# Dilated attention: products of identity by identity ahead of and inside its four calls

## The reference, cut to what matters

```python
ATTN_GROUPS = ((128, 1), (512, 4), (2048, 16))    # window, dilation; 8 heads of 64 in each group
def dilated_mixer(h, cos, sin, w_q, k_sh, v_sh, w_o):
    q = apply_rope_2((h @ w_q).reshape(B, S, 3, 8, 64), cos, sin)
    for g, (window, dilation) in enumerate(ATTN_GROUPS):
        o, l = dilated_window_attention(q[:, :, g], k_sh[:, :, g], v_sh[:, :, g], window, dilation)
    wts = softmax(stack(lses), axis=0)
    o = sum(wts[..., None] * stack(outs), axis=0)
    return o.reshape(B, S, O_WIDTH) @ w_o
```

## Time and profile before

| | |
|---|---|
| median of 3 runs | 3644.28 us (3637.61 to 3644.98) |
| the profiled execution | 3640.77 us |
| its span, first to last instruction | 3639.0 us |
| TensorE busy | 3385.7 us, 93% |
| VectorE busy | 1957.4 us, 54% |
| ScalarE busy | 1400.2 us, 38% |
| DMA | 107 GB/s, mean over the span |
| mean granted TensorE clock | 0.941 of 2.4 GHz |

### The profile page before, as it was taken

How to read it: one execution, slowest core, us unless ns; L and a number is a source line. 1 busy time by engine, 2 the same in 40 slices (tenths; PEclk the granted TensorE clock), 3 DMA queues, 4 the chain that set the end, 5 groups by cost and what they waited for, 6 DMA issues and landing times.

```text
span 3639.0 us, 41894 instructions
## 1 busy us (share of the span) xinstructions
PE 3385.7 (93%) x14724; PEld 2639.8 (73%) x14724; DVE 1957.4 (54%) x3052; ACT 1400.2 (38%) x2056; POOL 384.3 (11%) x233
## 2 busy tenths in 40 slices
PE   7799898997998898999997999999999989889998
PEld 5567677775676777788875788877887767668886
DVE  4753687557536876554546543456354443455353
ACT  3443567534434666322222322233223444432221
POOL 2101032322010222200010100010001000010000
PEclk9869999998598999999999999999999999899999
DMA  3101399611011998132322232324233212013232
GB/s 114 50 1 59 105 318 317 217 50 55 1 59 58 307 318 271 50 98 91 100 64 66 74 103 88 99 70 143 92 97 117 87 35 70 24 50 101 92 95 78
DMA packets 174980, 389.59 MB, mean 107 GB/s; under 512 B 11312, under 2 KB 70064, under 8 KB 174192
## 3 DMA queue, kind: packets, MB, share of 16 engines
q1 hardware_dynamic: 173424, 377.45, 32.3%
q0 software_dynamic: 1408, 10.23, 0.8%
HBM read 381.34 MB, written 6.29 MB: 107 GB/s over the span
## 4 chain that ended last, share of the span: by engine, by line
PE 71%; DVE 12%; DMA 8%; ACT 5%; DVEq 2%; issue 2%; POOL 0%; POOLq 0%; ACTq 0%; SPq 0%
PE ps L545 18%; PE ps L547 18%; PE ps L546 18%; DMA gate_up_stage<-in_w_gu 8%; PE ps L659 4%; DVE moe_lo L1809 4%; PE ps L681 3%; PE ps L665 2%; ACT moe_hi L1048 2%; PE ps L761 2%; PE ps L636 1%; PE ps L724 1%; PE ps L627 1%; ACT w_hi L1048 1%; PE ps L829 1%
## 5 line engine op out<-in xcount | busy, mean ns | idle before, releaser
L1466 DVE TENSOR_TENSOR w_lo<-w_stage,w_hi 128x1024 fp32r<-128x1024 f32 (+3 forms) x310 | 398.3, 1287 | 833.9 <-ACT w_hi L1048 832.8
L545 PE MATMUL ps<-xs_hi,w_hi 128*128 128x512 f32 (+2 forms) x1952 | 778.9, 399 | 53.2 <-DVE w_lo L1466 17.7
L1048 ACT ACTIVATE w_hi<-w_stage 128x1024 fp32r<-128x1024 f32 (+3 forms) x350 | 382.0, 1093 | 1032.3 <-PE ps L547 1020.9
L547 PE MATMUL ps<-xs_hi,w_lo 128*128 128x512 f32 (+2 forms) x1952 | 771.2, 395 | 0.0
L546 PE MATMUL ps<-xs_lo,w_hi 128*128 128x512 f32 (+2 forms) x1952 | 771.0, 395 | 0.0
L545 PEld LDWEIGHTS ps<-xs_hi,w_hi 128*128 128x128 f32 (+2 forms) x1952 | 369.1, 189 | 155.1 <-issue 39.1
L547 PEld LDWEIGHTS ps<-xs_hi,w_lo 128*128 128x128 f32 (+2 forms) x1952 | 368.8, 189 | 85.8
L546 PEld LDWEIGHTS ps<-xs_lo,w_hi 128*128 128x128 f32 (+2 forms) x1952 | 370.0, 190 | 82.9
L1809 DVE TENSOR_TENSOR moe_lo<-gate_up_stage,moe_hi 128x1024 fp32r<-128x1024 f32 x224 | 270.1, 1246 | 125.0 <-ACT moe_hi L1048 124.6
L1048 ACT ACTIVATE moe_hi<-gate_up_stage 128x1024 fp32r<-128x1024 f32 x224 | 226.6, 1053 | 147.6 <-DMA gate_up_stage<-in_w_gu 141.2
L547 PE MATMUL ps<-h_hi,w_lo 128*128 128x512 f32 x704 | 278.1, 395 | 0.0
(11 more groups left out here) (346 smaller groups left out, 5105.5 us busy)
## 6 DMA issues: line engine op xcount, KB each, us to landing
gate_up_stage<-in_w_gu SPq DMA_DIRECT2D x112, 1024.0 KB, 5.8
w_stage<-in_f_gu SPq DMA_DIRECT2D x174, 512.0 KB, 3.6
down_stage<-in_w_dn SPq DMA_DIRECT2D x112, 512.0 KB, 6.1
w_stage<-in_f_dn SPq DMA_DIRECT2D x64, 704.0 KB, 4.0
w_stage<-in_w_in SPq DMA_DIRECT2D x30, 512.0 KB, 3.6
w_stage<-in_d_qk SPq DMA_DIRECT2D x24, 512.0 KB, 3.5
w_stage<-in_w_out SPq DMA_DIRECT2D x16, 512.0 KB, 3.5
w_stage<-in_d_v SPq DMA_DIRECT2D x12, 512.0 KB, 3.6
```

Source lines behind the costliest of these rows:

```text
L545: pe.matmul(o, lh, rh, start=start, stop=False)
L547: return pe.matmul(o, ll, rh, start=False, stop=stop)
L1048: copy = lambda o, i: nc.scalar.activation(o, i, ACT.Copy)
L1466: tt(w_lo[:, s, 0:n], stage[:, s, 0:n], w_hi[:, s, 0:n].bitcast(F32), ALU.subtract).then_inc(w_split, 1)
```

## The change

`keep_clock` gets a third argument, the width w in tiles of 128 columns; its default leaves it as it was. Three calls are added in the dilated attention, all into bank 6:

- five products ahead of each call of `attend_wide`, before the wait for `heads_ready`. At e = 0 the wait for the last `act_copied` now stands ahead of them too, since bank 6 is one of those that the turned values are copied from;
- three products behind the scores of units 0 and 1;
- one product of 256 columns in each unit, ahead of the wait for `p_norm`.

```diff
-            def keep_clock(n, b=7):
+            def keep_clock(n, b=7, w=NT):
 
                 for _ in range(n):
-                    pe.matmul(ps[:, b, :], ident[:, :], ident[:, :].unsqueeze(1).to_broadcast([P, NT, P]), start=True, stop=True)
+                    pe.matmul(ps[:, b, 0:w * P], ident[:, :], ident[:, :].unsqueeze(1).to_broadcast([P, w, P]), start=True, stop=True)
...
                 for n in range(2):
                     scores(U[n], n, D_BANKS)
+                keep_clock(3, 6)
                 for n in range(N):
                     un, nb = U[n], U[n]["W"] // P
+                    keep_clock(1, 6, 2)
                     pe.wait_ge(p_norm, d0 + n + 1)
                     transposes(un, n, dprob, 6, D_RING)
...
                                 turn(2 * L + n_v + i - 1, (i - 1) % 2, P, 6 + (i - 1) % 2)
+                        if e == 0:
+                            pe.wait_ge(act_copied, L * COPIES + n_v + 6)
+                        keep_clock(5, 6)
                         pe.wait_ge(heads_ready, n_rope + 6 * e + 6)
                         pe.wait_ge(act_copied, L * COPIES + n_v + 6)
```

## The result

| | median | runs |
|---|---|---|
| before | 3640.47 us | 12 (3634.14 to 3646.03) |
| changed | 3651.06 us | 12 (3635.92 to 3659.01) |

The ratio is 1.0031, 95% interval 1.0019 to 1.0044: 11 us slower (7 to 16). The profiled execution took 3648.63 us, its span is 3646.9 us, 7.9 more than the 3639.0 of before.

A forecast was written before the change was run, and what follows sets the result against it. TensorE, busy for 93% of the span, was taken as the bound. Added products cost 24.0 us, the held clock gives back 17.2, a net loss of 6.8; one or two falls at e = 1 make +12: 3654 us (3645 to 3663).

The forecast's parts named there:

- No slack in units 1 to 5: Middle units of each call: TensorE waits for nothing, so narrow products cost 5 x 0.43 = 2.15 us per call.
- The faster rival: Units paced by VectorE and ScalarE, narrow products in slack, five at e = 0 overlapped: -11.8 us, 3629; chance 0.05.
- The five at e = 0 exposed: Ahead of the e = 0 calls, behind the last `dv` wait: 4.3 us exposed, twice, 8.6 us; the clock holds.
- The three and one: Between first scores and first transposes: 3.0 us of products where 1.65 were idle, 1.35 us exposed per call.
- What the clock can give: All four calls at full clock without added products: 35.0 us each, 140.0 against 157.2, so 17.2 us at most.
- The clock at e = 1: Heads of the e = 1 calls: one or two falls, 6.8 us low and 3.4 lost each; forecast chance 0.62.
- The rule of the Trainium skill: Rival at e = 1: the 1.4 us gap left is harmless, clock holds, +6.8 us, 3647.6; chance 0.18.

The follow-up runs named there:

- again: The changed kernel unaltered, measured once more on one chip beside the fitted kernel: median 3648.24 us, ratio to before 1.0023.
- the fitted kernel: Against the changed kernel, products only where TensorE was idle, no more than each gap holds, none in the units: ratio to before 0.9964, later 0.9952.
- both fitted forms: The fitted kernel, and the same with one narrow product added in each of units 1 to 7; the latter's ratio to before 0.9966, later 0.9975.

## Why the prediction was right

The forecast was 3654 us (3645 to 3663) and slower; 3651.06 and 1.0031 were measured.

- **No slack in units 1 to 5.** Right: 4.24 us for a unit. This step decided the sign. The faster rival hung on slack that the earlier trace rows didn't show, and the narrow products alone made the kernel slower. Their price was put at 0.43 us and is 0.48 (4.24 - 3.76): the two records take 0.54 us from start to start, and the transposes behind them run 0.06 faster. Per call 3.1 us came, as worked out of it.
- **The five at e = 0 exposed.** Right, 4.49 us for 4.3. That the clock holds there was right in the first call and wrong in the third, where it was low from the first of the five on and they took 6.15 us. Over the profiles with these five and the three behind (changed, again, without narrow products) that is one fall in six.
- **The three and one.** Transposes 5.92 us behind the scores for 6.05: the scores of two units take 2.80 us, not 3.05. A call at the full clock is 38.96 us for 38.8.
- **What the clock can give.** 35.0 us per call was worked out for a call with no added product at the full clock; the fitted kernel has 35.00 to 35.17. This term carries the reading that all four could gain 17 us and that the products cost more than that.
- **The clock at e = 1.** One fall in the first profile, one in the second, 6.8 us low and 3.3 us lost each, for 6.8 and 3.4. With the clock held throughout the sum would be 2 x (4.49 + 38.96) + 2 x 38.97 = 164.8, +7.6 for the forecast +6.8; two falls (3.3 at e = 1, 1.7 in the five) make it 12.6, for +12.
- **One reading too high.** The prediction says that a third of each call or more is spent at 1.2 GHz. In the first call it is 10.2 of 38.4 us, a little over a quarter; no term of the sum used this.
- **The rule of the Trainium skill** ("TensorE: Matmul & The Clock Gate", section "Why this matters for your kernels", that long idle gaps bring a mid-kernel fall) would have the clock held with 1.50 us of gap left. The trace disagrees: it fell there in six of eight e = 1 calls with the five and the three (changed twice, without the narrow ones, without the five at e = 0), and in the run with 64 rows behind a gap of 1.48 us. By these rows a gap of 1.5 us can be enough.
- **By luck:** that the sum of the clock's part came out so close, 12.6 for 12. The forecast put one or two falls at e = 1 and none at e = 0. The profile has one at e = 1 and one in the five at e = 0, together 5.0 us, where one or two of the expected kind were priced at 3.4 or 6.8. The second profile, with one fall at e = 1 alone, gives +11.0. Also the estimate on the profile's own time, 3652.8, was nearer than the 3654 that leaned on the median of three; with 12 runs the median of before is 3640.47.

## What to carry to other kernels

Filler on TensorE is free only up to the length of the wait that it stands in, and only ahead of the wait: read the gap in the timeline, divide by the measured start-to-start time of a record, and leave the last few tenths open. Behind the last wait, or in a loop whose groups start back to back, each product is paid in full: here 24 us of exposed products bought 12 us of clock, where 18 us of them inside the gaps bought 17. Where a bank with a pending reader forces filler behind a wait, look for a bank without one.

## What the runs showed of the hardware that was not expected

- Products over 64 rows did less to hold the 2.4 GHz than products over 128, in the same place and with as many columns: behind the same wait of 1.48 us, ten records over 64 rows ended at 1.2 GHz in two calls of two, ten over 128 rows in none of eight. The 64 rows rest on one profile.
- A fall can come behind the gap, while TensorE is busy: 1.5 us into the scores behind a wait of 1.50 us (second call of the changed kernel), 2.5 us into the five products over 64 rows behind 1.48 us. With the five products ahead and nothing behind the scores, the clock fell at the end of the scores in one call, in the wait behind them in two, and at the first transposes in one.
- Even with 0.65 us of gap ahead of the scores the clock fell in one e = 1 call of eight (both fitted forms, twice each), at 0.6 us lost (38.89 for 38.30).
- One kernel's medians over 12 and 17 runs on one chip can lie 7.7 us (0.2%) apart, and its first scores came at 2893.06 and at 2887.08 us: in the stages ahead the clock was at 1.2 GHz for 355 us in the one profile and for 314 in the other.
